# B heads' projection of a two-layer encoder: rotary rows of four heads in one unit ahead of unit 6, plain query units ahead of unit 7, values token-major

## The chip, the cores and the metric

The kernel runs on one core of a Trainium2 chip. The metric is device time in microseconds, from start to end of one execution; the median of several executions is given. An execution that is profiled leaves a trace of every instruction on TensorE (PE, with its weight loads PEld), VectorE (DVE), ScalarE (ACT), GpSimd (POOL) and of the DMA issues of SyncE (SP), with the time for which each waited and what ended the wait.

## The reference, cut to what matters

Two layers of an encoder on 1024 tokens of 1024 features. Each normalises, projects, runs four kinds of attention (A, B, C, D, four heads each), mixes, and adds a feed-forward block. The change lies in the projection of the B heads:

```python
def mla(u, cq_gain, ckv_gain, w_uq, w_ukv, ang_seq):
    c_q, c_kv, k_rope = jnp.split(u, [MLA_Q_RANK, MLA_Q_RANK + MLA_KV_RANK], axis=-1)      # 192, 128, 32 columns
    q = (rms_norm(c_q, cq_gain) @ w_uq).reshape(b, s, N_HEADS_B, MLA_NOPE + MLA_ROPE)      # 4 heads, 64 + 32
    kv = (rms_norm(c_kv, ckv_gain) @ w_ukv).reshape(b, s, N_HEADS_B, MLA_NOPE + MLA_V)     # 4 heads, 64 + 64
    q_nope, q_rope = jnp.split(q, [MLA_NOPE], axis=-1)
    k_nope, v = jnp.split(kv, [MLA_NOPE], axis=-1)
    q_rope = apply_rope(q_rope, ang_seq)      # x * cos + (halves swapped) * sin
    k_rope = apply_rope(k_rope, ang_seq)      # one for all four heads
    ...
    sc = (q_nope k_nope^T + q_rope k_rope^T) * (MLA_NOPE + MLA_ROPE) ** -0.5, softmax, times v
```

## The kernel before

Every float32 operand is split into a high part, rounded to the multiplier's width, and a low part, the rest; a product is then three matmuls (high by high, high by low, low by high). ScalarE writes high parts (functions that end in `_high`), VectorE or GpSimd low parts (`_low`). `part_products` (line 204) makes one such product of 128 output rows by 1024 tokens: six matmuls of 512 columns.

A layer is a row of stages with a barrier of all engines between them (`end_stage`, line 150). `projection_stage` (line 331) is the first stage of a layer and attention A the next. It has three parts. First the token-major rows: A's heads, then the latent columns of B (which are turned to feature-major and split into `b_h`, `b_l` (trace: `b_src_h`, `b_src_l`); rows 0 to 191 of them, in blocks 0 and 1, are the query latent, rows 64 to 96 of block 1 the rotary key, block 2 the key-value latent), then the values of C and D. Second, units 0 to 7: queries and keys of C and D, feature-major, 48 matmuls each, into one of two halves of the PSUM tile `u_ps` (`unit_out`); each is split (`p_h`, `p_l`) and spilled to DRAM by SP. Third, the B heads, one after the other, behind unit 7:

- TensorE: a query unit per head (`wq` has the head's 64 plain columns, 32 rotary ones and the same 32 with halves swapped, so 128 output rows), a key-value unit per head (64 key rows, 64 value rows), and eight transposes that turn the values to token-major (`turn_values`).
- ScalarE: copies both units to SBUF (`query_out` into `bh_u_q`, `key_value_out` into `bh_u_kv`), writes the high parts of keys, values and queries.
- GpSimd multiplies the swapped rows with the sine table (line 513, `bh_rt`), VectorE the rotary rows with the cosine table (line 854), and adds the two (line 856); then it writes the low parts of keys (860), values (865) and queries (870).
- SP copies the rotary key rows (`b_src_h`, `b_src_l`, partitions 64 to 96) under the keys of each head (line 479), eight copies of 128 KB, and waits for them (482).

The order of the work is the order in which it is written for each engine; semaphores tie the engines. The tiles `bh_u_q` and `bh_u_kv` lie in the memory of `p_h` and `p_l`, and so `query_out(0)` waits for the last spills. Heads share `unit_out(0)` and `unit_out(1)`, so the query unit of a head waits for the copy of the one before. B's queries and keys are stored where the normalised input was; the trace shows them as `h_hi` and `h_lo`.

## Time and profile before

| | us |
|---|---|
| median of 3 executions | 2993.41 (2992.62 to 2994.36) |
| profiled execution | 3001.38 |
| its span | 2999.2 |
| TensorE busy | 2735.2 (91%) |
| VectorE busy | 1916.9 (64%) |
| ScalarE busy | 1392.4 (46%) |
| GpSimd busy | 557.9 (19%) |

The mean granted clock of TensorE is 0.952 of full speed. How to read it: a busy share is an average over stages with different limits. TensorE is busy for most of the span, but what one edit is worth shows only in the stretch that it touches: which engine waits there, for whom, and what ends last ahead of the barrier. The stretch of the B heads comes twice, once a layer, near 268 and near 1745 us.

### The profile page before, as it was taken

The page shows a single profiled execution, that of the slowest core. Times are in us where ns is not written, and L with a number is a line of the kernel's source. Part 1 is how long each engine was busy: PE and PEld are TensorE (multiplying, and loading weights), DVE is VectorE, ACT ScalarE, POOL GpSimd, SP SyncE. Part 2 cuts the span into 40 slices and gives each one's busy share as a digit, 9 for nine tenths or more (in the row PEclk, how much of TensorE's full clock was granted, in tenths as well). Part 3 has the DMA queues.
Part 4 walks back from the last instruction along what each step waited for, and adds up shares of the span by engine and source line. Part 5 has one row for each costly group of instructions (what it writes and reads, how often), then busy time and mean ns, then how long its engine had stood idle before and what let it go on. Part 6 is the DMA issues. An engine that isn't in the chain of part 4 may idle for free. (4 is left out here: it accounts for less than half of the span.)

```text
span 2999.2 us, 37822 instructions
## 1 busy us (share of the span) xinstructions
PE 2735.2 (91%) x13872; PEld 2284.2 (76%) x13872; DVE 1916.9 (64%) x2792; ACT 1392.4 (46%) x2394; POOL 557.9 (19%) x487
## 2 busy tenths in 40 slices
PE   5999899888979999999879979989879799999997
PEld 4987789667758887888769859876768588878886
DVE  4612767886678887445674148669766877754467
ACT  4412766786343332443433137669754423234344
POOL 2122515790000000000022225249500000000000
PEclk8999999898989999999989999989989899999998
DMA  7232656543224444855533326654522244466565
GB/s 208 64 130 91 194 144 197 84 85 127 66 65 154 152 155 165 270 196 193 181 89 94 123 83 213 176 159 70 145 64 71 88 154 155 141 229 234 190 194 159
DMA packets 326943, 431.10 MB, mean 144 GB/s; under 512 B 82006, under 2 KB 207706, under 8 KB 326492
## 3 DMA queue, kind: packets, MB, share of 16 engines
q1 hardware_dynamic: 326736, 428.56, 47.1%
q8 instruction: 113, 1.85, 0.3%
q14 instruction: 82, 0.67, 0.1%
q10 hardware_dynamic: 12, 0.02, 0.0%
HBM read 288.00 MB, written 140.86 MB: 143 GB/s over the span
## 5 line engine op out<-in xcount | busy, mean ns | idle before, releaser
L2186 PE MATMUL f_ps<-dn_g 128*128 128x512 f32 x2688 | 621.3, 393 | 9.3 <-DVE dn_g L2417 9.2
L2186 PEld LDWEIGHTS f_ps<-dn_g 128*128 128x128 f32 x2688 | 508.4, 190 | 118.3 <-DVE dn_g L2417 6.8
L2417 DVE TENSOR_TENSOR dn_g<-dn_raw,dn_g 128x2048 fp32r<-128x2048 f32 x112 | 256.5, 2291 | 265.6 <-ACT dn_g L2266 265.5
L2176 PE MATMUL f_ps<-hc_h,up_w_h 128*128 128x512 f32 x896 | 352.1, 393 | 26.3 <-DVE up_w_l L2383 20.6
L2266 ACT ACTIVATE dn_g<-dn_raw 128x2048 fp32r<-128x2048 f32 x112 | 214.2, 1914 | 332.1 <-PE f_ps L2186 218.0
L2176 PE MATMUL f_ps<-hc_h,up_w_l 128*128 128x512 f32 x896 | 351.7, 393 | 0.0
L2176 PEld LDWEIGHTS f_ps<-hc_h,up_w_h 128*128 128x128 f32 x896 | 170.4, 190 | 63.0 <-DVE up_w_l L2383 27.8
L2176 PE MATMUL f_ps<-hc_ld,up_w_h 128*128 128x512 f32 x512 | 200.5, 392 | 0.0
L2176 PEld LDWEIGHTS f_ps<-hc_h,up_w_l 128*128 128x128 f32 x896 | 170.0, 190 | 35.9
L490 POOL TENSOR_TENSOR w_row_l<-w_row_first,w_row_h 128x512 fp32r<-128x512 f32 x12 | 14.9, 1275 | 898.7 <-ACT w_row_h L599 898.7
L1285 DVE CUSTOM_DVE_ANT_0 s_ps_c<-s_ps_c,distance 128x1024 f32<-128x1024 f32 x128 | 156.8, 1227 | 14.3 <-PE s_ps_c L1158 14.2
L1268 POOL TENSOR_TENSOR first_c<-first_c,second_c 128x1024 f32<-128x1024 f32 x64 | 152.7, 2385 | 5.3
L2176 PE MATMUL f_ps<-hc_lf,up_w_h 128*128 128x512 f32 x384 | 151.3, 394 | 0.0
L2246 ACT ACTIVATE up_w_h<-up_raw 128x512 fp32r<-128x512 f32 x96 | 60.4, 631 | 158.5 <-PE f_ps L2176 158.5
L1158 PE MATMUL s_ps_c<-c_k_s,c_q_s 128*128 128x512 f32 x256 | 101.1, 481 | 31.0 <-ACT first_c L1219 26.6
L522 PE MATMUL u_ps_p<-w_row_h,h_hi 128*128 128x512 f32 x256 | 104.5, 408 | 20.8 <-POOL w_row_l L490 20.8
L1077 DVE TENSOR_REDUCE nmax_b<-s_ps_b 128x1 f32<-128x1024 f32 x64 | 78.4, 1224 | 63.0 <-PE s_ps_b L966 62.9
L2176 PEld LDWEIGHTS f_ps<-hc_ld,up_w_h 128*128 128x128 f32 x512 | 96.8, 189 | 20.3
L2246 ACT ACTIVATE up_w_h<-up_s 128x512 fp32r<-128x512 f32 x128 | 80.0, 627 | 54.6 <-PE f_ps L2176 46.6
L522 PE MATMUL u_ps_p<-w_row_l,h_hi 128*128 128x512 f32 x256 | 102.4, 400 | 0.0
L522 PE MATMUL u_ps_p<-w_row_h,h_lo 128*128 128x512 f32 x256 | 102.1, 399 | 0.0
L1077 DVE TENSOR_REDUCE nmax_a<-s_ps_a 128x1 f32<-128x1024 f32 x64 | 78.3, 1223 | 34.7 <-PE s_ps_a L966 34.6
(297 smaller groups left out, 6461.8 us busy)
## 6 DMA issues: line engine op xcount, KB each, us to landing
act_blocks<-u_stage SPq DMA_DIRECT2D x32, 1792.0 KB, 6.6
dn_raw<-act_blocks SPq DMA_DIRECT2D x112, 512.0 KB, 4.0
mix<-in_w_down SPq DMA_DIRECT2D x128, 256.0 KB, 3.7
down_sums<-mix SPq DMA_DIRECT2D x128, 256.0 KB, 2.8
up_raw<-in_w_up SPq DMA_DIRECT2D x32, 1024.0 KB, 5.3
dn_raw<-down_sums SPq DMA_DIRECT2D x64, 512.0 KB, 5.2
dn_raw<-in_w_down SPq DMA_DIRECT2D x48, 512.0 KB, 4.6
w_raw<-in_w_in SPq DMA_DIRECT2D x16, 512.0 KB, 4.3
```

Of the source, the lines that this page charges most:

```text
L490: nc.gpsimd.tensor_tensor(lo[:, r % KT, :], row_source(r), hi[:, r % KT, :], ALU.subtract).then_inc(S["row_lo"], 1)
L522: last = nc.tensor.matmul(u_ps[:, i % 4, 0:n], x[:, k, tokens(i)], wt[:, k, :], start=(k == 0 and x is h_hi and wt is hi), stop=(k == KT - ...
L1077: nc.vector.tensor_reduce(nmax[:, n:n + 1], s, AX_X, ALU.max, negate=True) \
L1158: last = nc.tensor.matmul(s_ps[:, r, at:at + HALF], q(n % NT), k(at, at + HALF), start=True, stop=True)
L1268: nc.gpsimd.tensor_tensor(first[:, n % 3, :], first[:, n % 3, :], second[:, n % 2, :], ALU.add).then_inc(S["combined"], 1)
L1285: nc.vector.tensor_tensor_reduce(out=s_ps[:, r, :], in0=s_ps[:, r, :], in1=bias(n % NT), scale=SLOPES[n // NT], scalar=MIN_START, op0=ALU. ...
L2176: last = nc.tensor.matmul(dst, wt[:, x % RING, k, :], tok, start=(opens[j] and k == 0 and i == 0), stop=(k == KT // 2 - 1 and i == 2), ski ...
L2186: last = nc.tensor.matmul(f_ps[:, bank0[pi] + i, :], lhs[:, n % 4, 0, q, i * P:(i + 1) * P], rhs[:, n % 4, 1, q, :], start=(down_opens[pi] ...
L2246: nc.scalar.activation(w_h[:, x % RING], weight_block(x), ACT.Copy).then_inc(S["w_hi"], 1)
L2266: nc.scalar.activation(g_h[:, n % 4], dn_raw[:, n % 3], ACT.Copy).then_inc(S["d_hi"], 1)
L2417: nc.vector.tensor_tensor(g_l[:, n % 4], dn_raw[:, n % 3], g_h[:, n % 4], ALU.subtract) \
```

## The change

The weights of B's query projection are loaded in another order: block columns 0 and 1 hold the plain columns of heads 0, 1 and of heads 2, 3; column 2 holds the rotary columns of all four heads (32 each), column 3 the same with halves swapped. The key-value weights are split in the same way into two units of keys (two heads each) and 256 columns of values. The query projection then is four units: two rotary ones ahead of unit 6 and two plain ones ahead of unit 7, both into the PSUM tile `t_ps`, which is otherwise used for transposes. VectorE turns the rotary rows of all heads at once (`rope`: three instructions of 128 rows) and splits them during the units. Behind unit 7 stand two key units, and values as token-major products (`value_tiles`: 24 matmuls of 256 columns), which need no transposes. Splits of queries and keys are per head, 64 rows each; values are split in two halves of four token tiles. The rotary query rows lie head under head on 128 partitions, and SP copies them to partitions 64 to 96 of each head: eight copies of 128 KB more. The rotary key rows go in two copies of 512 KB instead of eight of 128 KB. The rotary table is loaded eight times (each quarter of the partitions, cosine and sine). GpSimd has no part in the third phase any more.

VectorE, from the splits of units 6 and 7 to the end of the stage. `bh_u_q` is the query unit of a head, `h_lo` the low part of queries and keys, `b_v_s` the values. Before:

```order
L847 SCALAR_TENSOR_TENSOR p_l<-u_ps_p,p_h 128x1024
L844 TENSOR_TENSOR p_l<-u_ps_p,p_h 128x1024
L854 TENSOR_TENSOR bh_u_q<-bh_u_q,cos_sin 32x1024
L856 TENSOR_TENSOR bh_u_q<-bh_u_q,bh_rt 32x1024
L860 TENSOR_TENSOR h_lo<-u_ps_p,h_hi 64x1024
L854 TENSOR_TENSOR bh_u_q<-bh_u_q,cos_sin 32x1024
L856 TENSOR_TENSOR bh_u_q<-bh_u_q,bh_rt 32x1024
L860 TENSOR_TENSOR h_lo<-u_ps_p,h_hi 64x1024
L865 TENSOR_TENSOR b_v_s<-t_ps_p,b_v_s 128x8x64
L870 TENSOR_TENSOR h_lo<-bh_u_q,h_hi 96x1024
```

and so on for heads 2 and 3, 20 instructions behind unit 7's split (L844). Now:

```order
L872 SCALAR_TENSOR_TENSOR bh_roped<-t_ps_p,cos_sin 128x1024
L874 SCALAR_TENSOR_TENSOR t_ps_p<-t_ps_p,cos_sin 128x1024
L876 TENSOR_TENSOR bh_roped<-bh_roped,t_ps_p 128x1024
L881 TENSOR_TENSOR bh_rope_l<-bh_roped,bh_rope_h 128x1024
L865 SCALAR_TENSOR_TENSOR p_l<-u_ps_p,p_h 128x1024
L862 TENSOR_TENSOR p_l<-u_ps_p,p_h 128x1024
L886 SCALAR_TENSOR_TENSOR h_lo<-t_ps_p,h_hi 64x1024 x2
L893 TENSOR_TENSOR h_lo<-u_ps_p,h_hi 64x1024 x2
L886 SCALAR_TENSOR_TENSOR h_lo<-t_ps_p,h_hi 64x1024 x2
L898 TENSOR_TENSOR b_v_s<-t_ps_p,b_v_s 128x4x4x64
L893 TENSOR_TENSOR h_lo<-u_ps_p,h_hi 64x1024 x2
L898 TENSOR_TENSOR b_v_s<-u_ps_p,b_v_s 128x4x4x64
```

The eight rotary passes of 32 rows became three of 128, ahead of unit 6's split; behind unit 7's split (L862 now) stand ten instructions.

SP, from the spill of unit 7 to the end of the stage. Before:

```order
L438 DMA cd_qk<-p_h 128x1024
L438 DMA cd_qk<-p_l 128x1024
L479 DMA h_hi<-b_src_h 32x1024
L479 DMA h_lo<-b_src_l 32x1024
L479 DMA h_hi<-b_src_h 32x1024
L479 DMA h_lo<-b_src_l 32x1024
L479 DMA h_hi<-b_src_h 32x1024
L479 DMA h_lo<-b_src_l 32x1024
L479 DMA h_hi<-b_src_h 32x1024
L479 DMA h_lo<-b_src_l 32x1024
```

Now (`bh_rope_h` and `bh_rope_l` are the rotary query rows):

```order
L442 DMA cd_qk<-p_h 128x1024
L442 DMA cd_qk<-p_l 128x1024
L492 DMA h_hi<-b_src_h 32x4x1024
L492 DMA h_lo<-b_src_l 32x4x1024
L498 DMA h_hi<-bh_rope_h 32x1024
L498 DMA h_lo<-bh_rope_l 32x1024
L498 DMA h_hi<-bh_rope_h 32x1024
L498 DMA h_lo<-bh_rope_l 32x1024
L498 DMA h_hi<-bh_rope_h 32x1024
L498 DMA h_lo<-bh_rope_l 32x1024
L498 DMA h_hi<-bh_rope_h 32x1024
L498 DMA h_lo<-bh_rope_l 32x1024
```

The key rows are two issues, and the eight copies of query rows are new behind them. The diff, cut to its core:

```diff
-        for d0, d1, c0 in ((0, QK, 0), (QK, QK + half, HD + half), (QK + half, P, HD)):
-            sp.dma_start(bw_raw[0:rows, k, :, d0:d1], wq[k * P:k * P + rows, :, c0:c0 + d1 - d0]) \
-                .then_inc(S["copy_landed"], 16)
-    sp.dma_start(bw_raw[:, 2, :, :], wkv).then_inc(S["copy_landed"], 16)
+        q_rows = wq[k * P:k * P + rows]
+        nope = bw_raw[0:rows, k, 0:2, :].rearrange("p u (h d) -> p (u h) d", h=2)
+        rope = bw_raw[0:rows, k, 2, :].rearrange("p (e d) -> p e d", e=NHEAD)
+        swap = bw_raw[0:rows, k, 3, :].rearrange("p (e d) -> p e d", e=NHEAD)
+        sp.dma_start(nope, q_rows[:, :, 0:HD]).then_inc(S["copy_landed"], 16)
+        sp.dma_start(rope, q_rows[:, :, HD:QK]).then_inc(S["copy_landed"], 16)
+        sp.dma_start(swap[:, :, 0:half], q_rows[:, :, HD + half:QK]).then_inc(S["copy_landed"], 16)
+        sp.dma_start(swap[:, :, half:B_ROPE], q_rows[:, :, HD:HD + half]).then_inc(S["copy_landed"], 16)
+    for j in range(2):
+        sp.dma_start(bw_raw[:, 2, 2 * j:2 * j + 2, :].rearrange("p u (h d) -> p (u h) d", h=2),
+                     wkv[:, :, j * HD:(j + 1) * HD]).then_inc(S["copy_landed"], 16)
...
-    sp.dma_start(cs[HD:P, :], a["cos_sin_b"]).then_inc(S["table_landed"], 16)
+    for j in range(2):
+        for e in range(NHEAD):
+            sp.dma_start(cs[e * B_ROPE:(e + 1) * B_ROPE, j, :],
+                         a["cos_sin_b"][j * B_ROPE:(j + 1) * B_ROPE, :]).then_inc(S["table_landed"], 16)
...
+    for dst, part in ((B["k_h"], b_h), (B["k_l"], b_l)):
+        sp.dma_start(dst[R0:R1, :, :].bitcast(F32),
+                     part[R0:R1, 1, :].bitcast(F32).unsqueeze(1).to_broadcast([B_ROPE, NHEAD, SEQ])) \
+            .then_inc(S["stack_landed"], 16)
+    sp.wait_ge(S["rope_lo"], 1)
     for e in range(NHEAD):
-        for dst, part in ((B["k_h"], b_h), (B["k_l"], b_l)):
-            sp.dma_start(dst[R0:R1, e, :].bitcast(F32), part[R0:R1, 1, :].bitcast(F32)).then_inc(S["stack_landed"], 16)
+        for dst, part in ((B["q_h"], rope_h), (B["q_l"], rope_l)):
+            sp.dma_start(dst[R0:R1, e, :].bitcast(F32), part[e * B_ROPE:(e + 1) * B_ROPE, :].bitcast(F32)) \
+                .then_inc(S["stack_landed"], 16)
     for j in range(2):
         sp.wait_ge(S[f"spilled{j}"], 2 * 16 * 4)
-    sp.wait_ge(S["stack_landed"], 16 * 2 * NHEAD)
+    sp.wait_ge(S["stack_landed"], 16 * (2 + 2 * NHEAD))
...
+    def query_unit(j, dst):
+        for k in range(2):
+            rows = w_rows[k]
+            last = part_products(dst, bw_h[0:rows, k, j, :], bw_l[0:rows, k, j, :],
+                                 b_h[0:rows, k, :], b_l[0:rows, k, :], k == 0, k == 1)
+        return last
+
+    def key_unit(j, dst):
+        return part_products(dst, bw_h[:, 2, j, :], bw_l[:, 2, j, :], b_h[:, 2, :], b_l[:, 2, :], True, True)
+
+    def value_tiles(g, dst):
+        wv_h, wv_l = (w[:, 2, 2:4, :].rearrange("p u d -> p (u d)") for w in (bw_h, bw_l))
+        for i in range(4):
+            out_cols = dst[:, i * 2 * P:(i + 1) * 2 * P]
+            for x, wt in ((b_h, wv_h), (b_h, wv_l), (b_l, wv_h)):
+                last = nc.tensor.matmul(out_cols, x[:, 2, tokens(4 * g + i)], wt,
+                                        start=(x is b_h and wt is wv_h), stop=(x is b_l))
+        return last
+
     for u in range(8):
+        if u == 6:
+            pe.wait_ge(S["bw_lo"], 3)
+            pe.wait_ge(S["back_lo"], 2 * NT)
+            query_unit(2, t_ps[:, 0, :])
+            query_unit(3, t_ps[:, 1, :]).then_inc(S["rope_gemm"], 1)
+        if u == 7:
+            pe.wait_ge(S["rope_done"], 1)
+            for j in range(2):
+                query_unit(j, t_ps[:, j, :]).then_inc(S["q_gemm"], 1)
...
-    for e in range(NHEAD):
-        if e:
-            pe.wait_ge(S["q_out"], e)
-        for k in range(2):
-            rows = w_rows[k]
-            last = part_products(unit_out(0), bw_h[0:rows, k, e, :], bw_l[0:rows, k, e, :],
-                                 b_h[0:rows, k, :], b_l[0:rows, k, :], k == 0, k == 1)
-        last.then_inc(S["q_gemm"], 1)
-        if e:
-            turn_values(e - 1)
-            pe.wait_ge(S["k_lo"], e)
-        else:
-            pe.wait_ge(S["lo_done"], 8)
-        part_products(unit_out(1), bw_h[:, 2, e, :], bw_l[:, 2, e, :], b_h[:, 2, :],
-                      b_l[:, 2, :], True, True).then_inc(S["kv_gemm"], 1)
-    turn_values(NHEAD - 1)
+    for j in range(2):
+        pe.wait_ge(S["lo_done"], 7 + j)
+        key_unit(j, unit_out(j)).then_inc(S["kv_gemm"], 1)
+    pe.wait_ge(S["q_lo"], 2)
+    value_tiles(0, t_ps[:, 0, :]).then_inc(S["tt_done"], 1)
+    pe.wait_ge(S["k_lo"], 2)
+    value_tiles(1, unit_out(0)).then_inc(S["tt_done"], 1)
...
+    def rope_high():
+        act.wait_ge(S["rope_done"], 1)
+        nc.scalar.activation(rope_h[:, :], roped[:, :], ACT.Copy).then_inc(S["rope_hi"], 1)
+    def query_high(e):
+        act.wait_ge(S["q_gemm"], e // 2 + 1)
+        act.wait_ge(S["gemm_done"], 8)
+        nc.scalar.activation(B["q_h"][0:HD, e, :], t_ps[e % 2 * HD:(e % 2 + 1) * HD, e // 2, :], ACT.Copy,
+                             scale=QK ** -0.5).then_inc(S["q_hi"], 1)
+    def key_high(e):
+        act.wait_ge(S["kv_gemm"], e // 2 + 1)
+        nc.scalar.activation(B["k_h"][0:HD, e, :], unit_out(e // 2)[e % 2 * HD:(e % 2 + 1) * HD], ACT.Copy) \
+            .then_inc(S["k_hi"], 1)
...
+        if u == 5:
+            rope_high()
+    query_high(0)
+    query_high(1)
+    key_high(0)
+    key_high(1)
+    query_high(2)
+    query_high(3)
+    head_values_high(0)
+    key_high(2)
+    key_high(3)
+    head_values_high(1)
...
+    def rope():
+        dve.wait_ge(S["table_landed"], 16 * 2 * NHEAD)
+        dve.wait_ge(S["rope_gemm"], 1)
+        counted(nc.vector.scalar_tensor_tensor(out=roped[:, :], in0=t_ps[:, 0, :], scalar=QK ** -0.5,
+                                               in1=cs[:, 0, :], op0=ALU.mult, op1=ALU.mult))
+        after(nc.vector.scalar_tensor_tensor(out=t_ps[:, 1, :], in0=t_ps[:, 1, :], scalar=QK ** -0.5,
+                                             in1=cs[:, 1, :], op0=ALU.mult, op1=ALU.mult))
+        nc.vector.tensor_tensor(roped[:, :], roped[:, :], t_ps[:, 1, :], ALU.add) \
+            .then_inc(S["rope_done"], 1)
+
+    def rope_low():
+        dve.wait_ge(S["rope_hi"], 1)
+        nc.vector.tensor_tensor(rope_l[:, :], roped[:, :], rope_h[:, :], ALU.subtract) \
+            .then_inc(S["rope_lo"], 1)
+
+    def query_low(e):
+        dve.wait_ge(S["q_hi"], e + 1)
+        nc.vector.scalar_tensor_tensor(out=B["q_l"][0:HD, e, :],
+                                       in0=t_ps[e % 2 * HD:(e % 2 + 1) * HD, e // 2, :], scalar=QK ** -0.5,
+                                       in1=B["q_h"][0:HD, e, :], op0=ALU.mult, op1=ALU.subtract) \
+            .then_inc(S["q_lo"], 1)
...
+        if u == 5:
+            rope()
+            rope_low()
+    query_low(0)
+    query_low(1)
+    key_low(0)
+    key_low(1)
+    query_low(2)
+    query_low(3)
+    head_values_low(0)
+    key_low(2)
+    key_low(3)
+    head_values_low(1)
```

## Rows read from the trace of the kernel before

**Rows 1.** Table of stretches: stretch, length, busy time (instructions) per engine, clock, DMA.

```profile
core 0: us, PE busy (x) PEld busy (x) DVE busy (x) ACT busy (x) POOL busy (x), PEclk, DMA share, GB/s
268.10:311.56 43.46, 27.31 (x106) 19.11 (x104) 22.75 (x21) 18.34 (x22) 13.59 (x4) 0.77 0.18 48
1745.35:1787.51 42.16, 24.54 (x106) 16.75 (x104) 24.61 (x21) 18.34 (x22) 12.56 (x4) 0.87 0.19 50
```

**Rows 2.** Timeline of TensorE, layer 0: start, duration, instruction, [idle before <- releaser].

```profile
268.07 0.39 PE L210 MATMUL u_ps_p<-b_src_h,bh_w_h 128*128 128x512 f32 x1
...
275.93 0.79 PE L210 MATMUL u_ps_p<-b_src_h,bh_w_h 128*128 128x512 f32 x1 [3.17 <-ACT bh_u_q L675]
...
311.56 0.76 PE L966 MATMUL s_ps_a<-a_k_s,a_q_h 128*128 128x512 f32 x1 [8.37 <-PEq L151]
```

**Rows 3.** Timeline of TensorE, layer 1, the first query unit and the next stage.

```profile
1745.35 0.39 PE L210 MATMUL u_ps_p<-b_src_h,bh_w_h 128*128 128x512 f32 x1
...
1746.81 0.49 PE L210 MATMUL u_ps_p<-b_src_h,bh_w_h 64*128 64x512 f32 x1
...
1748.39 0.50 PE L210 MATMUL u_ps_p<-b_src_h,bh_w_h 128*128 128x512 f32 x1
...
1787.51 0.76 PE L966 MATMUL s_ps_a<-a_k_s,a_q_h 128*128 128x512 f32 x1 [8.85 <-PEq L151]
```

**Rows 4.** Groups of instructions, 268 to 311: busy, mean ns, idle before and releasers.

```profile
L856 DVE TENSOR_TENSOR bh_u_q<-bh_u_q,bh_rt 32x1024 f32<-32x1024 f32 x4 | 4.9, 1217 | 9.3 <-POOL bh_rt L513 9.3
...
L675 ACT ACTIVATE bh_u_q<-u_ps_p 128x1024 f32<-128x1024 f32 x4 | 4.1, 1023 | 15.9 <-DVE h_lo L870 6.3 <-DMA cd_qk<-p_l 5.6 <-PE u_ps_p L214 4.1
```

**Rows 5.** Timeline of VectorE, layer 0: unit 7's split and the end of the stage.

```profile
269.33 1.23 DVE L844 TENSOR_TENSOR p_l<-u_ps_p,p_h 128x1024 fp32r<-128x1024 f32 x1 [9.66 <-ACT p_h L665]
...
305.47 1.22 DVE L860 TENSOR_TENSOR h_lo<-u_ps_p,h_hi 64x1024 fp32r<-64x1024 f32 x1
306.61 0.67 DVE L865 TENSOR_TENSOR b_v_s<-t_ps_p,b_v_s 128x512 fp32r<-128x512 f32 x1
...
308.94 1.21 DVE L870 TENSOR_TENSOR h_lo<-bh_u_q,h_hi 96x1024 fp32r<-96x1024 f32 x1
```

**Rows 6.** Timeline of ScalarE, layer 0: the evacuation of units 6 and 7.

```profile
257.39 1.03 ACT L665 ACTIVATE p_h<-u_ps_p 128x1024 fp32r<-128x1024 f32 x1 [8.91 <-PE u_ps_p L214]
268.27 1.03 ACT L665 ACTIVATE p_h<-u_ps_p 128x1024 fp32r<-128x1024 f32 x1 [9.85 <-PE u_ps_p L214]
```

**Rows 7.** Timeline of SP, layer 0: weights of B, rotary table, first spill.

```profile
126.40 5.12 SPq L458 DMA_DIRECT2D bh_w_raw<-in_b_w_uq  x6
131.70 0.46 SPq L460 DMA_DIRECT2D bh_w_raw<-in_b_w_ukv  x1
136.75 1.01 SPq L428 DMA_DIRECT2D w_raw<-in_w_in  x2
...
185.25 0.52 SPq L471 DMA_DIRECT2D cos_sin<-in_cos_sin_b  x1
...
194.57 0.32 SPq L438 DMA_DIRECT2D cd_qk<-p_h  x1
```

**Rows 8.** Timeline of SP, layer 0: spill of unit 7 and key rows.

```profile
270.58 0.32 SPq L438 DMA_DIRECT2D cd_qk<-p_h  x1
270.94 0.43 SPq L438 DMA_DIRECT2D cd_qk<-p_l  x1
...
271.42 0.80 SPq L479 DMA_DIRECT2D h_hi<-b_src_h  x1
...
276.94 0.59 SPq L479 DMA_DIRECT2D h_lo<-b_src_l  x1
```

**Rows 9.** SP's waits, 268 to 312: total, times, longest.

```profile
SPq L482 <- DMA h_lo<-b_src_l: 2.3, 1, 2.3
```

**Rows 10.** Table of stretches: the spill of unit 7, the eight key copies.

```profile
271.00:274.00 3.00, 1.76 (x7) 1.05 (x6) 0.00 (x0) 0.00 (x0) 0.00 (x0) 1.00 0.89 347
274.00:279.20 5.20, 3.27 (x7) 2.24 (x8) 1.22 (x1) 2.84 (x3) 3.18 (x1) 0.58 0.97 204
```

More of the change, by code:

```diff
@@ L104 @@
  s_done hc_hi hc_lo p1_copied p5_copied p7_added relu11 posts_done staged u_stored0 u_stored1
- lam_scaled lam_done evac_done taken tile_done final_done""".split()
+ rope_gemm rope_hi rope_lo lam_scaled lam_done evac_done taken tile_done final_done""".split()
 class Sems:
@@ L345, in projection_stage @@
                 st_l = st.take("p_l", [P, 2, SEQ], F32R)
-                st = arena((48, 64))
-                u_q = st.take("bh_u_q", [P, 2, SEQ])
-                u_kv = st.take("bh_u_kv", [P, 2, SEQ])
                 bw = arena((64, 80))
@@ L351, in projection_stage @@
                 bw_l = bw.take("bh_w_l", [P, 3, NHEAD, P], F32R)
+                rope_h = bw.take("bh_rope_h", [P, SEQ], F32R)
                 w2 = arena((80, 104))
@@ L358, in projection_stage @@
                 u_l = ring.take("w_l", [P, 2, KT, P], F32R)
-                rt = arena((96, 104)).take("bh_rt", [P, 2, SEQ])
                 src = arena((104, 128))
@@ L376, in projection_stage @@
                 bw_raw = arena((128, 134)).take("bh_w_raw", [P, 3, NHEAD, P])
+                roped = arena((128, 132)).take("bh_roped", [P, SEQ])
+                rope_l = arena((128, 132)).take("bh_rope_l", [P, SEQ], F32R)
                 vt = arena((134, 142)).take("v_out", [P, 2, 2 * NHEAD, P], F32R)
@@ L385, in projection_stage @@
                 xb = bt.take("b_xn", [P, 2, 3 * P])
-                cs = arena((134, 142)).take("cos_sin", [P, SEQ])
+                cs = arena((134, 142)).take("cos_sin", [P, 2, SEQ])
                 small = arena((142, TOP))
@@ L666, in unit_high @@
                             .then_inc(S["hi_done"], 1)
-                    def query_out(e):
-                        act.wait_ge(S["q_gemm"], e + 1)
-                        if e == 0:
-                            for j in range(2):
-                                act.wait_ge(S[f"spilled{j}"], 2 * 16 * 4)
-                        if e >= 2:
-                            act.wait_ge(S["q_lo"], e - 1)
-                        nc.scalar.activation(u_q[:, e % 2, :], unit_out(0), ACT.Copy, scale=QK ** -0.5) \
-                            .then_inc(S["q_out"], 1)
@@ L719, in _ @@
                         if t == 3:
[L720 removed]
+                            act.wait_ge(S["copy_landed"], 16 * 10)
                         if t == NT - 1:
```

76 lines of the change are left out of this document (13 added, 63 removed).

## The prediction

> **What bounds the kernel now.** I first took the table of stretches and looked at the two places that the diff touches: from the first product behind unit 7 to the first score of attention A, 43.5 us in the first layer and 42.2 us in the second [rows 1]. TensorE is busy for only 27.3 and 24.5 us of them, and no engine is busy for all of it: each head goes in a ring, where TensorE, ScalarE, GpSimd and VectorE wait for one another. I call the start of that stretch T: 268.07 in layer 0, 1745.35 in layer 1 [rows 2, 3]. The groups of that stretch say who waits [rows 4]: ScalarE sits 15.9 us ahead of its four copies of the query unit, 5.6 of them for the spill of unit 7, and VectorE 9.3 us for GpSimd's rotary product. The stage ends when VectorE's last split is out, at 308.94 + 1.21 = 310.15; 1.41 us behind it the next stage's first product starts [rows 2, 5]. So the bound is a dependency chain, and what the change is worth is the length of this tail against what is put ahead of T. Everything outside the two stretches and outside units 5 to 7 is untouched. There is a barrier at the end of the stage, so a microsecond taken from the tail is a microsecond of the kernel.
>
> **Part 1, what goes ahead of T.** Two rotary units ahead of unit 6, two plain query units ahead of unit 7, all on TensorE. A query unit is twelve products of 512 columns, six over 128 rows and six over 64. In layer 1 the first one runs from 1745.35 to 1748.39, that is 3.04 us, at full clock and with no wait [rows 3]. The first product after a change of row count costs 0.10 us more (0.49 against 0.39 in its row, [rows 3]). Four units and their restarts: 4 x 3.04 + 0.3 = 12.5 us per layer. TensorE has no idle time between units (unit 7's evacuation starts 10.88 us behind unit 6's, 257.39 to 268.27 [rows 6], and a unit has 48 products), so all 12.5 us are on the path. I take it at full clock, since TensorE comes out of units that keep it busy.
>
> Could it wait there? Unit 7's query units wait for the rotary sum. The rotary products end 6.3 us behind unit 5. VectorE then makes three passes of 1024 columns at 1.23 us or less each [rows 5] with a wait between, some 4 us: ready 10.3 us behind unit 5, needed 6.3 + 10.9 = 17.2 us behind it. The split of the rotary rows (1.0 us ScalarE, 1.2 us VectorE) comes next and is over before unit 6's evacuation. Their cover is unit 6, with 7 us to spare; it costs nothing. If the cover were gone, the 4 us of VectorE would be added.
>
> **Part 2, SP's new transfers ahead.** Ten weight loads in place of seven. The six of before took 5.12 us to issue from 126.40, and SP's next wait ends only at 136.75 [rows 7]. Three more at 5.12 / 6 = 0.85 us each add 2.6 us to 132.2 and end before 134.8: nothing. The rotary table is eight loads of 128 KB behind the value spills, where one issue stood at 185.25; at 0.6 us each as the head copies [rows 8], SP is through near 190.1. SP's next job, the spill of unit 0, starts at 194.57 [rows 7]. Nothing again.
>
> **Part 3, what leaves the tail.** The whole ring: four copies of query units, four of key-value units, eight rotary passes on VectorE and four on GpSimd, 32 transposes. The wait of ScalarE for unit 7's spill (5.6 us [rows 4]) goes too, since nothing reuses the spilled tile.
>
> **Part 4, what the tail is then, engine by engine, from T' = T + 12.5.**
> TensorE: key unit 0 at once, key unit 1 when VectorE has split unit 7 (the split ends at 270.56 = T + 2.5 [rows 5]), then 24 products of 256 columns. At 0.23 us each, the pace of twice as wide ones, they are 5.5 us; even at half clock they wait for VectorE and not the other way round.
> ScalarE: eleven copies of 1.0 us, paced by 0.9: done before T' + 11.
> VectorE: unit 7's split starts at 269.33 = T + 1.26 [rows 5]. Behind it stand four query splits, four key splits and two value splits of 1024 columns. All read PSUM; such a split takes 1.22 us, and the next starts 1.14 us behind it (305.47 to 306.61 [rows 5]). So 1.26 + 11 x 1.14 + 0.08 = **T' + 13.9**.
> SP and the DMA queues: this is the part that the list of engines hides. Before, the eight copies of the rotary key rows (128 KB each) stood behind the spill of unit 7: last issue at 276.94 + 0.59, SP's wait 2.3 us more, so over at 279.83 = T + 11.8 [rows 8, 9]. It was hidden under a tail of 42 us. The key copies stay (two of 512 KB in place of eight of 128 KB, the same 1.05 MB), and eight copies of the rotary query rows come behind them, another 1.05 MB, since SP issues them only after the key copies. Rate: the queues were saturated. The spill's stretch shows 347 GB/s at a DMA share of 0.89, the copies' stretch 204 GB/s at 0.97 [rows 10]. The new copies write the same 32 partitions (64 to 96) in rows of 4 KB, so I take 204 GB/s: 1.05 MB / 204 GB/s = 5.1 us. SP is over at **T' + 16.9**, 3 us after VectorE. The end of the stage changes hands from VectorE to the DMA queues.
>
> **The sum.** New stretch, from T to the next stage's first product: 12.5 + 16.9 + 1.4 = 30.8 us. Before: 43.5 and 42.2. Gain 12.7 + 11.4 = 24.1 us. The profiled execution (3001.4 us, span 2999.2) would become 2977.3; it lies 8.0 us above the median of the three timed runs, 2993.4, so the forecast for the median is **2969.3 us**.
>
> **Rivals.**
> A, the query copies are no limit and VectorE is. For it: their sources are rows 0 to 127 and not the written ones, and 347 GB/s shows in the same queue. At that rate they take 3.0 us and end at T' + 14.8; if the key copies, now two large ones, go fast too, the tail is VectorE's T' + 13.9. Gain 3.0 us more per layer: 2963.3. Against it: the written partitions are the same.
> B, the copies are slower than I take: eight issues that each follow the other with new sources, 130 GB/s say, 8.1 us and not 5.1. It gives 2 x 3.0 less gain: 2975.3.
> C, the change doesn't do all that it says: TensorE waits ahead of unit 6 or 7 after all, or the moved products run at half clock for some of their time (in this trace the clock fell to half where TensorE stood for 3.17 us ahead of 275.93 [rows 2]). One such wait of 3.2 us and 3 us of products at half clock cost 4.7 us per layer: 2978.7. Against it: every wait there has 7 us to spare.
> D, slower than before. One mechanism: copies between different partition groups in the tail. The trace has none, only copies from a partition to itself; if they were paced by reading one port and writing another, the rate could be far from 204. It decides at the point where the gain of 12 us per layer is eaten, so when the query copies take 5.1 + 12 = 17.1 us, 61 GB/s. At 50 GB/s they take 21 us, and the kernel 2969.3 + 2 x 15.9 = 3001.1. Against it: the loads and spills of this trace read and write quite different places at over 200 GB/s.
>
> **How the numbers follow.** Forecast 0.60, A 0.16, B 0.11, C 0.09, D 0.04. Forecast, A and most of B hold more than 8 in 10; with what is unknown in each (0.5 us on the moved units, 1 us on the landing, twice) the range is 2961 to 2977. A measurement of this kernel tells 0.2% from no change, 6 us; a gain of 24 us is four times that. A, B, C and the forecast are all faster: 0.94. Between them and D the copies could land at the level of before: same 0.03. Slower 0.03.
>
> **What would show it.** In the profile after: four units of 3.0 us with no idle between units 5, 6 and 7; VectorE's rotary passes inside unit 6; GpSimd with nothing behind the last unit weight; VectorE's last value split 13.9 us behind the start of key unit 0, ScalarE's before 11. SP's last wait, on a rotary query copy, should end 3 us after VectorE, with about 200 GB/s over 10 us in the table of stretches. If VectorE ends last, A holds. If the copies' stretch shows under 150 GB/s, B or D. If an idle row stands ahead of the products into `t_ps`, or the granted clock falls ahead of T', C. What would make the prediction wrong outright is a stretch from key unit 0 to the next stage that is longer than 30 us.

## The result, and the profile after

| | before | changed |
|---|---|---|
| median of four runs | 2993.78 us | 2973.70 us |
| lowest to highest | 2992.62 to 2994.36 | 2972.54 to 2976.88 |
| profiled execution, its span | 3001.38, 2999.2 us | 2976.88, 2975.2 us |
| mean granted clock of TensorE | 0.952 | 0.953 |

The ratio of the times is 0.9934, with a 95% interval of 0.9921 to 0.9948: faster by 20.1 us. The forecast was 2969.3, the range 2961 to 2977.

T' is the first product behind unit 7: 279.45 in layer 0 and 1745.08 in layer 1. The table of stretches answers to [rows 1]. Its columns are those named there.

```profile
core 0: us, PE busy (x) PEld busy (x) DVE busy (x) ACT busy (x) POOL busy (x), PEclk, DMA share, GB/s
244.00:279.45 35.45, 35.45 (x150) 27.17 (x149) 7.26 (x6) 4.06 (x4) 2.39 (x1) 1.00 0.15 60
279.45:298.66 19.21, 6.57 (x38) 5.00 (x36) 13.26 (x11) 11.04 (x12) 0.00 (x0) 0.88 0.67 164
1745.08:1764.22 19.14, 6.57 (x37) 4.99 (x36) 13.26 (x11) 11.03 (x12) 0.00 (x0) 0.84 0.67 164
```

Ahead of T' TensorE is busy for the whole stretch at the full clock (1.00), so nothing waits at units 6 and 7. (Layer 1 takes the same time from unit 5's end to T'.) Behind it the tail, the time from T' to the next stage's first product, is 19.21 us in layer 0 and 19.14 in layer 1, where it was 43.5 and 42.2 [rows 1], and GpSimd has nothing in it. In the tail no compute engine is busy for more than 13.3 of the 19.2 us; the DMA share, 0.67, is the one number that has grown.

TensorE's timeline of layer 0 answers to [rows 2].

```profile
245.03 0.39 PE L210 MATMUL t_ps_p<-b_src_h,bh_w_h 128*128 128x512 f32 x1
...
279.45 0.39 PE L210 MATMUL u_ps_p<-b_src_h,bh_w_h 128*128 128x512 f32 x1
...
281.99 0.50 PE L210 MATMUL u_ps_p<-b_src_h,bh_w_h 128*128 128x512 f32 x1 [1.02 <-DVE p_l L862]
...
284.37 0.39 PE L581 MATMUL t_ps_p<-bh_w_h,b_src_h 128*128 128x256 f32 x1 [0.72 <-DVE h_lo L886]
...
298.66 0.77 PE L999 MATMUL s_ps_a<-a_k_s,a_q_h 128*128 128x512 f32 x1 [10.09 <-PEq L151]
```

The rotary units start at 245.03, where unit 5 ends. From there to T' are 34.42 us, against 21.76 before: **12.66 us were put ahead**, forecast 12.5. The last row shows the price of the tail: TensorE has done its products for 10.09 us when the barrier (L151) lets the next stage in.

VectorE's timeline of layer 0 answers to [rows 5].

```profile
251.42 1.23 DVE L872 SCALAR_TENSOR_TENSOR bh_roped<-t_ps_p,cos_sin 128x1024 f32<-128x1024 f32 x1 [3.91 <-PE t_ps_p L214]
...
256.17 1.23 DVE L881 TENSOR_TENSOR bh_rope_l<-bh_roped,bh_rope_h 128x1024 fp32r<-128x1024 f32 x1 [1.13 <-ACT bh_rope_h L691]
...
280.71 1.23 DVE L862 TENSOR_TENSOR p_l<-u_ps_p,p_h 128x1024 fp32r<-128x1024 f32 x1 [15.99 <-ACT p_h L686]
281.86 2.46 DVE L886 SCALAR_TENSOR_TENSOR h_lo<-t_ps_p,h_hi 64x1024 fp32r<-64x1024 f32 x2
...
289.36 1.23 DVE L898 TENSOR_TENSOR b_v_s<-t_ps_p,b_v_s 128x1024 fp32r<-128x1024 f32 x1
290.50 2.46 DVE L893 TENSOR_TENSOR h_lo<-u_ps_p,h_hi 64x1024 fp32r<-64x1024 f32 x2
293.00 1.23 DVE L898 TENSOR_TENSOR b_v_s<-u_ps_p,b_v_s 128x1024 fp32r<-128x1024 f32 x1
```

The rotary passes and their split lie inside unit 6 and are over at 257.4, 4.8 us before the plain units start at 262.24. From 280.71 on VectorE has no gap. Its last split ends at 294.23 = T' + 14.8 (forecast T' + 13.9).

SP's timeline of layer 0 and its wait at the end of the stage answer to [rows 8] and [rows 9].

```profile
281.97 0.32 SPq L442 DMA_DIRECT2D cd_qk<-p_h  x1
...
282.81 0.80 SPq L492 DMA_DIRECT2D h_hi<-b_src_h  x1
283.65 1.21 SPq L492 DMA_DIRECT2D h_lo<-b_src_l  x1
284.91 2.83 SPq L498 DMA_DIRECT2D h_hi<-bh_rope_h  x1
287.78 2.69 SPq L498 DMA_DIRECT2D h_lo<-bh_rope_l  x1
290.52 0.60 SPq L498 DMA_DIRECT2D h_hi<-bh_rope_h  x1
...
293.70 0.59 SPq L498 DMA_DIRECT2D h_lo<-bh_rope_l  x1
```

```profile
SPq L502 <- DMA h_lo<-bh_rope_l: 2.7, 1, 2.7
```

The last issue ends at 294.29 and SP waits about 2.8 us more for a rotary query copy to land: over at 297.1 = T' + 17.65 (forecast T' + 16.9), 2.9 us behind VectorE. Two of the query copies' issues last 2.83 and 2.69 us where the others last 0.6: SP is held up there, while the key copies are still under way. So the end of the stage has gone from VectorE to the DMA queues, as forecast.

The DMA view of 281 to 299 (40 slices of 0.45 us) shows the rates.

```profile
GB/s 0 0 0 36 391 410 410 419 382 364 200 173 218 173 173 173 200 155 191 173 191 173 191 346 237 228 219 191 228 164 219 209 128 27 0 0 0 0 0 0
```

The spill of unit 7 goes at about 400 GB/s until 285.5. The two key copies then go at about 180 and the eight query copies at about 215, until 296.3. This answers to the 347 and 204 of [rows 10].

**Where the 24.0 us between the two profiled spans lie.** From unit 5's end to the next stage's first product: 65.25 to 53.63 us in layer 0 and 63.92 to 53.56 in layer 1, so 11.62 + 10.36 = 21.98 us less. Attention A, the stage behind it, takes 1.58 us more in layer 0 (105.44 against 103.86), and the same 103.9 in layer 1. The rest of the kernel, whose work is nearly the same, is 1.29 + 1.61 + 0.74 = 3.64 us shorter by itself. That rest comes to 2662.3 us in the profile of before and 2658.7 in this one; in the ten other profiles of this study it lies between 2653.1 and 2659.6, and the profiled execution of before lay 8.0 us above its median. So the 3.6 us are put down to that one execution and not to the change. What the change makes of its own stretches and of attention A together is 22.0 - 1.6 = 20.4 us, and the medians show 20.1.

### The profile page after: what moved, and what is told of

It is laid out like the page before. It is cut to its first block and busy times, and to the rows that moved or that the text cites. A ratio compares the mean times of both kernels' runs of the same rounds, so it can differ in the third digit from the quotient of the medians.

```text
span 2975.2 us, 37716 instructions
## 1 busy us (share of the span) xinstructions
PE 2722.3 (92%) x13832; PEld 2276.1 (77%) x13832; DVE 1906.7 (64%) x2780; ACT 1380.7 (46%) x2376; POOL 531.5 (18%) x479
## 5 line engine op out<-in xcount | busy, mean ns | idle before, releaser
L1631 POOL TENSOR_TENSOR mix<-mix 128x256 f32<-128x256 f32 x64 | 47.1, 736 | 311.9 <-DMA mix<-in_w_down 311.7
```

The lines of the kernel that those rows point to most:

```text
L1631: nc.gpsimd.tensor_tensor(dst[:, 0, 0], raw[:, 0, 1], raw[:, 0, 0], ALU.subtract) \
```

## Experiments

The changed kernel was run again beside the first group. All kernels are edits of it. The kernel before had 2994.70 us with the first group (e0, e1, e3, e4), 2995.08 with the second (e2, e5, e6, e7) and 2995.03, from one run, with the third (e8, e9).

| kernel | median, us | ratio to before, 95% interval | tail from T', layers 0 and 1, us |
|---|---|---|---|
| e0 changed kernel again | 2974.44 | 0.9936, 0.9919 to 0.9952 | 19.17, 19.24 |
| e1 without the query copies | 2969.21 | 0.9920, 0.9903 to 0.9937 | 16.19, 16.20 |
| e2 key copies by head | 2973.93 (one run) | | 18.75, 18.81 |
| e3 copies ahead of the spill | 2968.61 | 0.9918, 0.9901 to 0.9934 | 17.12, 17.08 |
| e4 plain query units behind unit 7 | 2960.18 | 0.9886, 0.9869 to 0.9902 | 19.17, 19.18 |
| e5 products in TensorE's idle time | 2973.42 | 0.9927, 0.9910 to 0.9943 | 19.18, 19.35 |
| e6 e3 and e4 together | 2958.78 | 0.9877, 0.9860 to 0.9893 | 17.06, 17.08 |
| e7 e6 and e5 together | 2955.18 | 0.9862, 0.9845 to 0.9878 | 17.13, 17.14 |
| e8 query rows to 128 partitions | 2971.57 (one run) | | 17.62, 17.36 |
| e9 even heads adjacent | 2972.70 (one run) | | 19.21, 19.07 |

### e0, the changed kernel again

> The changed kernel as it is, on the same chip as the others, for their comparison, and for the second stage's start: in its first profile the attention stage of layer 0 took 105.4 us from first product to first product of the next stage, against 103.8 of before, with the granted clock at half for 8 us and not 4. If this comes from the longer idle time of TensorE ahead of the barrier (10.1 us in place of 8.4), it should be seen again in layer 0, 1.6 us. If it is chance, the two layers differ from profile to profile: in the first profile layer 1 took 103.9 us after 10.0 us of idle time. Time 2973.7.

Its tails are within 0.10 us of the first profile's, and in the five profiles whose tail should be the same (the changed kernel twice, e4, e5, e9) they lie between 19.07 and 19.35. A difference of 0.3 us or more that both layers show can thus be read from the tails, which the medians can't tell. Attention A again took 105.35 us in layer 0 and 103.86 in layer 1, so its longer time in layer 0 came back with the kernel.

### e1, without the query copies: do the queues set the end?

```diff
-                    for e in range(NHEAD):
-                        for dst, part in ((B["q_h"], rope_h), (B["q_l"], rope_l)):
-                            sp.dma_start(dst[R0:R1, e, :].bitcast(F32), part[e * B_ROPE:(e + 1) * B_ROPE, :].bitcast(F32)) \
...
-                    sp.wait_ge(S["stack_landed"], 16 * (2 + 2 * NHEAD))
+                    sp.wait_ge(S["stack_landed"], 16 * 2)
```

> The changed kernel without the eight copies of rotary query rows (so these rows of the queries hold old data and the result is not the reference's). Theory: the queues set the end of the stage. In the changed kernel SP's last wait ends 17.65 us behind the start of key unit 0 (T'), VectorE at T' + 14.8, and the next stage's first product starts at T' + 19.2. Without the copies the queues are through near T' + 12 and VectorE ends last: first product at T' + 14.8 + 1.5 = 16.3, 2.9 us less per layer, 5.8 us in all against the changed kernel, so about 2968 where the changed kernel has 2973.7. Rival: VectorE (or the barrier) sets the end as it is: nothing changes, 2973.7.

TensorE, layer 0, and SP's wait at the end of the stage:

```profile
276.47 0.39 PE L210 MATMUL u_ps_p<-b_src_h,bh_w_h 128*128 128x512 f32 x1
...
292.66 0.76 PE L994 MATMUL s_ps_a<-a_k_s,a_q_h 128*128 128x512 f32 x1 [7.08 <-PEq L151]
```

```profile
SPq L497 <- DMA h_lo<-b_src_l: 6.9, 1, 6.9
```

The tail is 16.19 us instead of 19.2, and SP is done 2.5 us before VectorE. So the copies are what ends last in the changed kernel, and they cost it 3.0 us per layer. That is rival A's state: the tails give the 6.0 us that A promised for free copies. The median shows 5.2 of them, with attention A long in both layers here (105.34 and 105.48 us) and in one of e0's.

### e2, the key copies head by head: does the repeating source cost time?

```diff
-                        sp.dma_start(dst[R0:R1, :, :].bitcast(F32),
-                                     part[R0:R1, 1, :].bitcast(F32).unsqueeze(1).to_broadcast([B_ROPE, NHEAD, SEQ])) \
+                    for e in range(NHEAD):
+                        for dst, part in ((B["k_h"], b_h), (B["k_l"], b_l)):
+                            sp.dma_start(dst[R0:R1, e, :].bitcast(F32), part[R0:R1, 1, :].bitcast(F32)).then_inc(S["stack_landed"], 16)
```

> The changed kernel with the rotary key rows copied as before, eight copies of 128 KB, instead of two of 512 KB that read one source four times. In the changed kernel the stretch of the key copies shows 183 GB/s and the one of the query copies 219 GB/s, and SP is over at T' + 17.65 where 16.9 was worked out from 204 GB/s for all. Theory: the form of the key copies costs the 0.75 us; with the old form SP is over at T' + 16.9 to 17.1 and the next first product stands at T' + 18.4 to 18.6 in place of 19.2. Rival: the rate is that of the written partitions whatever the form, and SP's end stays at T' + 17.5 to 17.8.

TensorE, layer 0, and SP's wait at the end of the stage:

```profile
274.55 0.39 PE L210 MATMUL u_ps_p<-b_src_h,bh_w_h 128*128 128x512 f32 x1
...
293.30 0.77 PE L998 MATMUL s_ps_a<-a_k_s,a_q_h 128*128 128x512 f32 x1 [9.64 <-PEq L151]
```

```profile
SPq L501 <- DMA h_lo<-bh_rope_l: 2.6, 1, 2.6
```

The tail is 0.3 to 0.5 us shorter, though SP issues sixteen copies in place of ten. SP is over at T' + 17.15 and not T' + 17.65. That lies between the theory's 16.9 to 17.1 and the rival's 17.5 to 17.8. So 0.4 to 0.5 us of the 0.75 by which SP ended later than forecast come with the form of the key copies: two large ones that read one source four times. Whether it is the repeated source or the size, this edit doesn't separate, and the rest of the 0.75 has no experiment. The long issues go with the large copies too: here no issue of a query copy lasts more than 0.66 us.

### e3, the copies ahead of the spill

```diff
-                    for u in range(8):
+                    for u in range(7):
                         spill_unit(u)
...
+                    spill_unit(7)
```

> The changed kernel with SP's order turned: key and query copies straight behind the last product of unit 7, the spill of unit 7 behind them. Theory (the queues are saturated from the spill to the end, so what counts is when their 3.15 MB start): the copies start at T' + 0.3 instead of T' + 3.3, the whole ends some 2.2 us earlier, near T' + 15.4, still just behind VectorE's T' + 14.8. First product 2.2 us earlier per layer, 4.4 us in all: about 2969.3. Rival: the copies' pace of 200 GB/s leaves no room and the spill is drawn out behind them, or its landing in DRAM takes longer than a copy's: less than 1 us per layer, about 2973.

SP and TensorE, layer 0:

```profile
277.83 0.74 SPq L492 DMA_DIRECT2D h_hi<-b_src_h  x1
...
288.58 0.46 SPq L442 DMA_DIRECT2D cd_qk<-p_l  x1
```

```profile
277.64 0.39 PE L210 MATMUL u_ps_p<-b_src_h,bh_w_h 128*128 128x512 f32 x1
...
294.76 0.77 PE L1000 MATMUL s_ps_a<-a_k_s,a_q_h 128*128 128x512 f32 x1 [8.00 <-PEq L151]
```

The first copy is issued 0.2 us behind T', where it was 3.4. The spill of unit 7 has to wait for VectorE's split (T' + 2.5); the copies need not, and in the changed kernel they stood behind it in SP's program. The same 3.15 MB now start earlier, SP is over at T' + 15.45 and the tail is 2.1 us shorter in both layers. It is still bound by the queues: VectorE ends 0.65 us earlier.

### e4, the plain query units behind unit 7

```diff
-                        if u == 7:
-                            pe.wait_ge(S["rope_done"], 1)
-                            for j in range(2):
-                                query_unit(j, t_ps[:, j, :]).then_inc(S["q_gemm"], 1)
...
+                    pe.wait_ge(S["rope_done"], 1)
                     for j in range(2):
...
                         key_unit(j, unit_out(j)).then_inc(S["kv_gemm"], 1)
+                        query_unit(j, t_ps[:, j, :]).then_inc(S["q_gemm"], 1)
```

ScalarE and VectorE take key heads 0 and 1 first, then query heads 0 and 1, and so on, and the values' two halves change places in PSUM.

> The changed kernel with the two plain query units taken from ahead of unit 7 to behind it, each behind a key unit; keys are split ahead of queries, values last. The rotary units stay ahead of unit 6. Theory: the 12.5 us of products ahead of key unit 0 are all on the path, and TensorE stands idle for 10 us of the tail, so 6.3 us per layer move under the copies, which end at T' + 17.65 as before. VectorE then ends near T' + 15 to 16, still ahead of the queues. 12.6 us less than the changed kernel, about 2961. Rival: VectorE, which now waits for query units, ends behind the copies, at T' + 20 or later: 7 us less at most, 2967 or more.

VectorE and TensorE, layer 0:

```profile
273.26 2.48 DVE L891 TENSOR_TENSOR h_lo<-u_ps_p,h_hi 64x1024 fp32r<-64x1024 f32 x2
276.20 2.47 DVE L884 SCALAR_TENSOR_TENSOR h_lo<-t_ps_p,h_hi 64x1024 fp32r<-64x1024 f32 x2 [0.47 <-ACT h_hi L694]
...
284.86 1.21 DVE L896 TENSOR_TENSOR b_v_s<-t_ps_p,b_v_s 128x1024 fp32r<-128x1024 f32 x1
```

```profile
270.64 0.39 PE L210 MATMUL u_ps_p<-b_src_h,bh_w_h 128*128 128x512 f32 x1
...
289.81 0.77 PE L997 MATMUL s_ps_a<-a_k_s,a_q_h 128*128 128x512 f32 x1 [7.10 <-PEq L151]
```

This is the largest single step, 14.3 us under the changed kernel. From unit 5's end to T' are 28.09 us in place of 34.42, so the two plain units' 6.3 us leave the path, and the tail stays at 19.17 us, since they fit into the time in which TensorE stood there. VectorE ends 0.6 us later (T' + 15.4), still ahead of the queues. Placing the plain units ahead of unit 7, which the change does, costs 12.7 us in the two layers that nothing asks for. Some 1.4 us of the rest are attention A's, which took 103.9 us in both layers here and 105.4 in one layer of the changed kernel.

### e5, products in TensorE's idle time

```diff
+                    pe.wait_ge(S["q_lo"], 4)
+                    for i in range(30):
+                        nc.tensor.matmul(t_ps[:, 1, 0:HALF], bw_h[:, 2, 0, :], b_h[:, 2, 0:HALF], start=True, stop=True)
```

The products' results are not used.

> The changed kernel with 30 products of 512 columns behind the value products, into a part of t_ps that nobody reads any more, from VectorE's last query split (T' + 9.9) to T' + 16.7, inside the time in which TensorE waits for the copies. Theory: the next stage's first products run at half clock (0.77 and 0.63 us in their rows where 0.50 and 0.40 is full clock) because TensorE was idle for 10 us; with the idle time cut to some 3 us they run at full clock, the first eight products take 0.23 us each and not 0.43, and the attention stage is 1.6 us shorter in each layer: about 2970.5. Rival: the clock falls within the barrier's gap anyway, and the stage keeps its two lengths, 103.9 and 105.4 us: 2973.7. The tail itself should stay at 19.2 us in both.

The tail is unchanged within 0.2 us. The next stage's first product now takes 0.47 us, not 0.77, and attention A 102.99 and 103.01 us, where e0 had 105.35 and 103.86. So the stage got shorter as the theory said, but the time did not follow: the median is 2973.42 where 2970.5 was expected. In these profiled runs the rest of the kernel gives 2.7 of those 3.2 us back. Its scatter between profiles is larger than that (2653.1 to 2659.6 us), so whether the rest pays for the products or this is chance stays open.

### e6 and e7, what adds up

e6 makes the edits of e3 and e4, and e7 adds 15 products of e5's kind behind VectorE's last key split.

> Both orders at once: plain query units behind the key units, and the copies ahead of the spill of unit 7. Theory: 6.3 us per layer less ahead of the tail as measured for the one (the time fell from 2974.4 to 2960.2), and the copies' end at T' + 15.5 as measured for the other; VectorE ends at T' + 15.4 as in the first of them, so both end together and the next first product stands at T' + 17.1: 4.1 us less than 2960.2, about 2956. Rival: with key and query splits bunched, VectorE or the copies slip behind each other, T' + 18 or later: 2958 or more.

> As the kernel with both orders, with 15 products of 512 columns behind the value products (into the PSUM of key unit 1, once its splits are out), T' + 12 to T' + 15.4. If idle time of TensorE ahead of the barrier makes the next stage's start slow, about 1.6 us less per layer than the kernel with both orders, near 2953; if the clock falls in the barrier's gap anyway, the same as that kernel.

In e6 SP and VectorE end together, both at T' + 15.4, so the two edits share a bound. In e1, where VectorE ended last, the next product came 1.42 us behind it; with its end at T' + 15.43 the tail can't fall under about 16.9. The expected time was missed by 2.8 us; attention A took 105.48 and 105.37 us, 3.0 us more than in e4's two layers. e7 takes that away. TensorE, layer 0, and the stage behind in the table of stretches:

```profile
284.48 3.59 PE L612 MATMUL u_ps_p<-b_src_h,bh_w_h 128*128 128x512 f32 x15
289.70 0.47 PE L1001 MATMUL s_ps_a<-a_k_s,a_q_h 128*128 128x512 f32 x1 [1.63 <-PEq L151]
```

```profile
289.70:392.69 102.99, 97.29 (x705) 88.14 (x705) 80.26 (x104) 76.93 (x145) 48.52 (x68) 1.00 0.56 174
```

The same stretch of the changed kernel:

```profile
298.66:404.10 105.44, 100.64 (x705) 90.97 (x705) 80.52 (x104) 77.06 (x145) 48.55 (x68) 0.95 0.54 170
```

The same 705 products are 3.35 us shorter in TensorE's busy time, at a mean granted clock of 1.00 and not 0.95. e7 has the lowest median of the study: 2955.18 us, 19.3 under the changed kernel's (e0) and 39.9 under the one before. Its 3.6 us under e6 are not clear of the noise, as the two intervals overlap, and of the 4.9 us that attention A gives in the two layers the rest of the kernel gives 3.0 back in these profiles, as in e5.

### e8, the query rows to 128 partitions

```diff
-                    for e in range(NHEAD):
-                        for dst, part in ((B["q_h"], rope_h), (B["q_l"], rope_l)):
-                            sp.dma_start(dst[R0:R1, e, :].bitcast(F32), part[e * B_ROPE:(e + 1) * B_ROPE, :].bitcast(F32)) \
...
+                    for j, part in enumerate((rope_h, rope_l)):
+                        sp.dma_start(spread_rows[:, j, :], part[:, :].bitcast(F32)).then_inc(S["stack_landed"], 16)
```

> The eight copies of query rows, each of 128 KB into 32 partitions, become two of 512 KB into the 128 partitions of a tile that nothing reads, so the same 1.05 MB are moved from the same rows and the query stacks keep old rotary rows (that part of the result is left out). Theory, that it is the 32 written partitions that hold these copies near 210 GB/s: the same bytes go at the 390 GB/s that the spill and key copies showed just before, in 2.7 us where they took 4.8, so SyncE is done some 2 us sooner, at T'+15.6, VectorE ends at T'+14.8 as before, and the next stage's first product is at T'+17.1. Rival, that copies from SBUF to SBUF run so slowly as such, because both ends are in one memory: the rate stays near 210 GB/s, SyncE is done at T'+17.6 and the first product stands at T'+19.2.

The DMA view of 277 to 292 (slices of 0.375 us):

```profile
GB/s 0 0 0 175 426 393 404 415 404 393 306 219 175 175 186 175 208 175 175 186 197 197 175 175 131 197 109 240 350 382 448 404 415 262 87 33 0 0 0 0
```

Three levels in one line: the spill at 400, the key copies into 32 partitions at 180 for about 6 us, then the query rows into 128 partitions at 400 for about 2.5 us. Both ends of the last are in SBUF, so copies from SBUF to SBUF are not slow as such and the rival falls. The size of a copy isn't it either: the key copies at 180 are two of 512 KB, like the query copies at 400. The Trainium skill says in its page "SBUF — State Buffer", section "Door 1: The DMA port swizzle", that 32 partitions reach eight of sixteen ports. The trace agrees, with about twice the rate where all 128 are reached. The edit widens the source and the target at once, and the query copies of the changed kernel read 32 partitions each as they write 32. So no run here says which of the two sides decides.

The tails were 17.62 and 17.36, not 17.1: in layer 0 the key copies landed about 0.8 us later than in the changed kernel, and the rate has a dip of an entry or two between the levels.

### e9, even heads adjacent: why do splits of 64 rows stand 1.25 us apart?

```diff
                     query_high(0)
-                    query_high(1)
                     key_high(0)
+                    query_high(1)
                     key_high(1)
```

The same on VectorE.

> ScalarE and VectorE take the heads in the order query 0, key 0, query 1, key 1 and then the rest as they were, nothing else. The time stays within 2 us of the changed kernel's, since the query copies set the stage's end. The question is why the splits of 64 rows stand 1.24 to 1.25 us apart on VectorE (ScalarE's copies 1.04) where those of 128 rows stood 1.14 (0.91). Theory, that an odd head's instruction, which reads partitions 64 to 127 and writes 0 to 63, does not overlap with its neighbours: the key 0 split, now behind query 0's and like it reading and writing 0 to 63, follows it by 1.14 (ScalarE by 0.91), all others by 1.25 (1.04). Rival, that 64 rows as such make the step longer, whatever partitions they are in: all are 1.24 to 1.25 (1.04) as before.

VectorE, layer 0: the splits of query 0, key 0, query 1, key 1, then query 2 and 3.

```profile
280.19 1.20 DVE L886 SCALAR_TENSOR_TENSOR h_lo<-t_ps_p,h_hi 64x1024 fp32r<-64x1024 f32 x1
281.32 1.20 DVE L893 TENSOR_TENSOR h_lo<-u_ps_p,h_hi 64x1024 fp32r<-64x1024 f32 x1
282.56 1.23 DVE L886 SCALAR_TENSOR_TENSOR h_lo<-t_ps_p,h_hi 64x1024 fp32r<-64x1024 f32 x1
283.70 1.22 DVE L893 TENSOR_TENSOR h_lo<-u_ps_p,h_hi 64x1024 fp32r<-64x1024 f32 x1
284.95 2.47 DVE L886 SCALAR_TENSOR_TENSOR h_lo<-t_ps_p,h_hi 64x1024 fp32r<-64x1024 f32 x2
```

The starts are 1.13, 1.24, 1.14 and 1.25 us apart. Neither theory is right as written. The rival falls, since 64 rows can follow each other in 1.13. My theory had key 1 behind query 1 (both odd, both reading partitions 64 to 127) at 1.25, and it is 1.14. What fits all four is the **change**: an instruction that reads the same half as the one before follows it after 1.13 to 1.14, and one that goes from even to odd head or back after 1.24 to 1.25. The PSUM tile changes at each of these four steps, so the tile isn't what differs. ScalarE shows the same in this run, starts of 0.90 and 0.92 us within a half, and 1.04 and 1.03 across. In the changed kernel every two neighbouring heads are of different halves; this order has two such steps fewer, and VectorE ends 0.2 us earlier (T' + 14.56, not 14.78). This reading was made after the result and was not put to another run.

## Why the prediction was right, and what was off in it

The mechanism held in the two stretches: one long ring of engines replaced by work ahead of T, and a short tail that the DMA queues end and not VectorE. e1 shows who ends the tail, and e4 what the work ahead of it costs. Which part of the change (the rotary rows at once, GpSimd's leaving, values without transposes) is worth how much of the shorter tail, no run takes apart. The sizes, layer 0:

| term | forecast | measured |
|---|---|---|
| four query units ahead of T | 12.5 | 12.66 |
| VectorE's end | T' + 13.9 | T' + 14.8 |
| SP's end | T' + 16.9 | T' + 17.65 |
| barrier to the next product | 1.4 | 1.56 |
| T to the next stage | 30.8 | 31.87 |

**Part 1** was short by 0.15. A unit that starts behind one of another row count pays the 0.10 restart too, so there are more than three per layer. The step from the last end to the next stage's product, 1.41 us behind VectorE before, was 1.56 behind SP now and adds another 0.15. Unit 6 covered VectorE's rotary work, with the clock at 1.00 and no idle row.

**Part 2 and 3** held. Nothing is late ahead of T', and GpSimd has left the stage.

**Part 4, VectorE**, was mis-sized: I took 1.14 from a pair in [rows 5] and used it for all eleven. Every pair of heads steps from one half of the partitions to the other, at 1.24 to 1.25. That is 0.9 us, and it changed nothing, because the queues end 2.9 us later. ScalarE was over at T' + 11.4, and not before 11, with 1.04 between such copies in place of 0.9.

**Part 4, the queues**, is the term that carries most of the miss in the tail: 0.75 us per layer. The rate of 204 GB/s was near that of the query copies (215). The two key copies went at 180; I had taken their end, T + 11.8, over from before, since they are the same bytes. e2 puts 0.4 to 0.5 of it on their form.

**The sum** is thus 1.06 us too small per layer: 21.98 us were gained in the two stretches, not 24.1.

**The stage behind** was put at nothing ("Everything outside the two stretches and outside units 5 to 7 is untouched"), and it wasn't: attention A took 1.58 us more in layer 0, and 1.49 more in e0. So of the 4.4 us between the forecast and the median, 2.1 are the stretches', about 1.6 are attention A's (if the timed executions had what both profiles show), 0.4 come from the median of before (2993.41 with three executions, 2993.78 with four), and 0.3 are not accounted for. That the forecast stayed inside its range doesn't make this step right.

The 8.0 us by which the profiled execution of before lay above its median had no part in this. They are added and taken off again: the forecast is the median of before less the gain. For a profiled execution they matter, and there luck was at work: 2977.3 was worked out and 2976.9 came, since 2.1 us too much gain in the stretches and 1.6 lost in attention A met 3.6 us by which the rest of the kernel was shorter in that one execution.

**The rivals.** A fell by the row of SP's wait and by e1. B fell, as the copies' two stretches show 183 GB/s (the key copies) and 219 (mostly the query copies), and not 130:

```profile
285.50:290.00 4.50, 2.26 (x17) 1.85 (x16) 4.38 (x5) 4.40 (x6) 0.00 (x0) 1.00 0.96 183
290.00:294.00 4.00, 0.00 (x0) 0.00 (x0) 3.94 (x4) 0.85 (x1) 0.00 (x0) 0.98 0.97 219
```

C fell, there is no idle time ahead of T'. D fell: copies between partition groups were the faster ones of the two kinds.

**What I missed** is that the place of the plain query units was a cost and not a need. I priced all 12.5 us and asked only whether TensorE would wait there. In the tail that I worked out myself, TensorE had some 10 us with nothing to do: e4 puts half of the 12.5 there and gets it back in full (6.3 us per layer).

## What to carry to other kernels

When a tail becomes short, work out who ends it, then ask which of the work just put ahead of it would fit into the engines that now stand idle in it: here two units of 3.1 us per layer did, for some 12.7 us of the kernel, where the whole change gave 20. Where DMA queues end a stage, look at what stands ahead of the copies in the issuing engine's program and what that waits for; issuing the copies first was worth 2.1 us per layer with no byte less. And look at the stage behind a tail that changes: here it took back 1.6 us of the gain, with the same instructions. A profiled execution is one execution (8.0 us above the median before, 3.2 after the change), so compare profiles stretch by stretch and not by their spans.
